# Matmul passes of the gate items, and the order of work at the start and end of each feed-forward block, in a two-layer fp32 decoder trunk

## The reference

```python
def swiglu(h, w_gate, w_up, w_down):
    return (jax.nn.silu(h @ w_gate) * (h @ w_up)) @ w_down

for l in range(DEPTH):                      # DEPTH = 2
    x = x + 0.5 * swiglu(rms_norm(x, g_ffn1[l]), w_ffn1_gate[l], w_ffn1_up[l], w_ffn1_down[l])
    h = rms_norm(x, g_mix[l])
    if l % 2 == 0:
        x = x + conv_gating_mixer(h, ...)   # causal convolution and spatial gating
    else:
        x = x + stick_breaking_mixer(h, w_qkv[i], w_o[i])   # 16 heads
    x = x + 0.5 * swiglu(rms_norm(x, g_ffn2[l]), w_ffn2_gate[l], w_ffn2_up[l], w_ffn2_down[l])
return rms_norm(x, g_final)
```

## Time and profile before

| | |
|---|---|
| Median of 3 runs | 1903.31 us (1903.06 to 1914.06) |
| The profiled execution | 1902.97 us, span of its instructions 1901.2 us |
| Mean granted TensorE clock | 0.993 of full speed |
| PE busy | 1843.3 us, 97% of the span, 11817 matmuls |
| PEld busy | 1646.3 us, 87% |
| DVE busy | 1408.8 us, 74% |
| ACT busy | 915.6 us, 48% |
| POOL busy | 504.6 us, 27% |
| DMA | 248.84 MB, mean 131 GB/s |

### The profile page before, as it was taken

One profiled execution on the slowest core, in us unless ns is written; L12 is line 12 of the kernel. 1 busy time (PEld: TensorE's weight loads), 2 busy tenths in 40 slices (PEclk: granted clock), 3 DMA queues, 4 the chain that ended last, 5 costly groups with the idle time before them and its releaser, 6 DMA issues.

```text
span 1901.2 us, 29396 instructions
## 1 busy us (share of the span) xinstructions
PE 1843.3 (97%) x11817; PEld 1646.3 (87%) x11817; DVE 1408.8 (74%) x1309; ACT 915.6 (48%) x1110; POOL 504.6 (27%) x379
## 2 busy tenths in 40 slices
PE   5999999999999999999999999999999999999997
PEld 5999988787779999887899988787888889999886
DVE  6797876589878888755888785654676688897753
ACT  6454544345274545444545453334565465455442
POOL 3344402201013433001344410221333224433021
PEclk8999999999999999999999999999999999999999
DMA  8788642232267886426778843222111277876321
GB/s 218 166 195 196 157 133 89 78 100 67 69 140 185 193 195 159 130 92 136 172 179 189 190 143 98 78 89 67 45 45 45 67 175 161 195 176 167 122 89 44
DMA packets 228250, 248.84 MB, mean 131 GB/s; under 512 B 7780, under 2 KB 196272, under 8 KB 227648
## 3 DMA queue, kind: packets, MB, share of 16 engines
q1 hardware_dynamic: 179232, 195.58, 34.0%
q0 software_dynamic: 48816, 51.98, 17.5%
q10 hardware_dynamic: 112, 0.03, 0.0%
HBM read 241.27 MB, written 2.10 MB: 128 GB/s over the span
## 4 chain that ended last, share of the span: by engine, by line
PE 74%; DVE 14%; issue 5%; ACT 3%; POOL 2%; DMA 1%; DVEq 0%; SPq 0%; ACTq 0%; POOLq 0%
PE ps L400 24%; PE ps L401 23%; PE ps L402 23%; DVE w_lo L1520 4%; DVE y L1814 2%; POOL chain L2144 2%; PE ps L903 1%; PE ps L897 1%; DVE xs_lo L1643 1%; ACT w_hi L1056 1%; DVE hid L1629 1%; DVE w_lo L1491 1%; PE ps L566 1%; DVE hid L1573 1%; DMA stage<-in_w_ffn_gate_dram 1%
## 5 line engine op out<-in xcount | busy, mean ns | idle before, releaser
L400 PE MATMUL ps<-xs_hi,w_hi 128*128 128x256 f32 (+1 forms) x3168 | 968.9, 306 | 37.3 <-DVE w_lo L1520 23.3
L401 PE MATMUL ps<-xs_lo,w_hi 128*128 128x256 f32 (+1 forms) x3168 | 963.8, 304 | 0.0
L402 PE MATMUL ps<-xs_hi,w_lo 128*128 128x256 f32 (+1 forms) x3168 | 963.6, 304 | 0.0
L400 PEld LDWEIGHTS ps<-xs_hi,w_hi 128*128 128x128 f32 x3168 | 598.5, 189 | 78.4 <-issue 30.9
L402 PEld LDWEIGHTS ps<-xs_hi,w_lo 128*128 128x128 f32 x3168 | 597.1, 188 | 31.9
L401 PEld LDWEIGHTS ps<-xs_lo,w_hi 128*128 128x128 f32 x3168 | 596.5, 188 | 32.4 <-issue 1.0
L1520 DVE TENSOR_TENSOR w_lo<-stage,w_hi 128x1024 fp32r<-128x1024 f32 x264 | 399.2, 1525 | 14.0 <-ACT w_hi L1056 13.0
L1056 ACT ACTIVATE w_hi<-stage 128x1024 fp32r<-128x1024 f32 x176 | 181.4, 1055 | 143.1 <-DMA stage<-in_w_ffn_gate_dram 74.0
L1643 DVE TENSOR_TENSOR xs_lo<-hid,xs_hi 128x1024 fp32r<-128x1024 f32 x88 | 110.5, 1255 | 176.0 <-ACT xs_hi L1176 176.0
L1520 DVE TENSOR_TENSOR w_lo<-chain,w_hi 128x1024 fp32r<-128x1024 f32 x132 | 160.9, 1219 | 87.3 <-ACT w_hi L1056 87.3
L1176 ACT ACTIVATE xs_hi<-hid 128x1024 fp32r<-128x1024 f32 x88 | 93.4, 1061 | 260.6 <-PE ps L402 254.7
(11 more groups left out here) (234 smaller groups left out, 2239.5 us busy)
## 6 DMA issues: line engine op xcount, KB each, us to landing
stage<-in_w_ffn_up_dram SPq DMA_DIRECT2D x88, 512.0 KB, 4.2
stage<-in_w_ffn_gate_dram SPq DMA_DIRECT2D x88, 512.0 KB, 6.2
stage<-in_w_ffn_down_dram SPq DMA_DIRECT2D x88, 512.0 KB, 3.8
chain<-in_w_ffn_gate_dram POOLq DMA_DIRECT2D x47, 512.0 KB, 7.5
stage<-in_w_ffn_gate_dram POOLq DMA_DIRECT2D x44, 512.0 KB, 8.8
chain<-in_w_ffn_up_dram SPq DMA_DIRECT2D x43, 512.0 KB, 7.4
stage<-in_w_qkv_dram SPq DMA_DIRECT2D x24, 512.0 KB, 4.7
stage<-in_w_in_ab_dram SPq DMA_DIRECT2D x16, 512.0 KB, 4.8
```

The lines of the kernel that those rows point to most:

```text
L400: pe.matmul(to, a_hi, b_hi, start=start, stop=False, skip_group_check=True)
L401: pe.matmul(to, a_hi, b_lo, start=False, stop=False, skip_group_check=True)
L402: return pe.matmul(to, a_lo, b_hi, start=False, stop=stop, skip_group_check=True)
```

## The change

1. **Gate items pass by pass.** `gate_part` becomes `gate_pass(..., part)`: part 0 is hi x hi for all t and k, part 1 is w_hi x xs_lo, part 2 is w_lo x xs_hi. `gate_item` waits for `item_hi_made` ahead of parts 0 and 1, and for `item_lo_made` only ahead of part 2. The number of matmuls stays.
2. **First step on PE.** `first_part` waits for each part on its own. The order was: W11 and T1 on tile groups 0 and 1, then W21 and T3 on tiles 0 to 2, then the last tile of all four. It is now: W11 and T1 on groups 0 and 1; T3 on tiles 0 to 2 (not in FFN 0); the last tile of T1 and W11; the rest of T3; all of W21.
3. **First step on ScalarE and VectorE** (`x_rest`, `gate_first`): T2 is split ahead of S2, v0 is copied and W22 split ahead of S4; T4's hi comes ahead of the squares of x tiles 4 to 7, which now follow T1 of step 1. In FFN 0 the copies of x tiles 4 to 7 move into `gate_first`. In FFN 1 and 3, T1 of step 0 is split earlier, between the x tiles.
4. **Step 2 on VectorE**: T3 and W21 of the next step are split at the end of a step, not at the start of the next; in `gate_second` they stand between `make_hid`, `c11` and `c22`.
5. **Down tail on PE**: outputs 4 and 5 are done row by row for the last two rows, outputs 6 and 7 as before.
6. **Attention on PE**: `suffix` runs on the hi half of `keep` before it waits for the lo half; `attend` runs its three passes over all key blocks in turn and waits for `prob_lo` only ahead of the last.

```diff
-            def gate_part(n, item, bank, ks):
+            def gate_pass(n, item, bank, ks, part):
 
                 slot = (RING_AT[n] + item) % RING
+                w, xs = (w_lo if part == 2 else w_hi), (xs_lo if part == 1 else xs_hi)
                 for t in range(2):
                     for k in ks:
...
+                        mm = pe.matmul(ps[:, bank + BANK_OF[item], t * HS:(t + 1) * HS],
+                                       w[:, slot, (2 * k + t) * P:(2 * k + t + 1) * P], xs[:, PART_OF[item], k, :],
...
             def gate_item(n, step, item):
 
-                pe.wait_ge(item_lo_made, step.count(ITEMS, n * FFN_ITEMS + item + 1))
+                pe.wait_ge(item_hi_made, step.count(ITEMS, n * FFN_ITEMS + item + 1))
...
-                gate_part(n, item, step.bank(n), range(KH)).then_inc(item_used, 1)
+                for part in range(2):
+                    gate_pass(n, item, step.bank(n), range(KH), part)
+                pe.wait_ge(item_lo_made, step.count(ITEMS, n * FFN_ITEMS + item + 1))
+                gate_pass(n, item, step.bank(n), range(KH), 2).then_inc(item_used, 1)
+
+            def first_part(n, item, ks, made):
+
+                bank = Step(0).bank(n)
+                pe.wait_ge(item_hi_made, n * FFN_ITEMS + item + 1)
+                pe.wait_ge(xs_hi_made, PARTS * n + made)
+                gate_pass(n, item, bank, ks, 0)
+                pe.wait_ge(xs_lo_made, PARTS * n + made)
+                gate_pass(n, item, bank, ks, 1)
+                pe.wait_ge(item_lo_made, n * FFN_ITEMS + item + 1)
+                return gate_pass(n, item, bank, ks, 2)
...
+                    first_part(n, W11, range(*PAIRS[g]), 2 * g + 1)
+                    first_part(n, T1, range(*PAIRS[g]), 2 * g + 2)
+                if n:
+                    first_part(n, T3, range(KH - 1), 2 * 2)
+                for item in (T1, W11):
+                    first_part(n, item, [KH - 1], 2 * len(PAIRS)).then_inc(item_used, 1)
+                first_part(n, T3, [KH - 1] if n else range(KH), 2 * len(PAIRS)).then_inc(item_used, 1)
+                first_part(n, W21, range(KH), 2 * len(PAIRS)).then_inc(item_used, 1)
...
-                for at in range(GROUP, DT):
+                for e in range(FT - TAIL, FT):
+                    down_ready(n, e)
+                    for at in range(GROUP, GROUP + 2):
+                        mm = down_item(n, e, at)
+                        if e == FT - 1:
+                            mm.then_inc(down_summed, 1)
+                for at in range(GROUP + 2, DT):
                     for e in range(FT - TAIL, FT):
...
-                pe.wait_ge(keep_lo_made, h + 1)
-                for part in (keep_hi, keep_lo):
+                for part, made in ((keep_hi, keep_hi_made), (keep_lo, keep_lo_made)):
+
+                    pe.wait_ge(made, h + 1)
```

More of the change, by code:

```diff
@@ L620, in gate_first @@
             def gate_first(n):
-                norm, step, bank = NORM_FFN[n], Step(0), Step(0).bank(n)
+                norm, step = NORM_FFN[n], Step(0)
                 pe.wait_ge(x_ready, norm * DT + GROUP)
                 for g in range(2):
[L625 to L637, removed]
@@ L639, in gate_first @@
+                for item in (T2, W22):
+                    pe.wait_ge(v0_copied if item == T2 else r0_copied, n * HF + 1)
+                    first_part(n, item, range(KH), 2 * len(PAIRS) + 1 + item - T2).then_inc(item_used, 1)
                 gate_item(n, step, T4)
@@ L1120, in gate_first @@
                 copy_r0(n, Step(0))
-                copy_v0(n, Step(0))
-                hi(n, Step(0), W22)
-                for j in range(GROUP, DT):
-                    x_square(n, j)
                 hi(n, Step(0), T4)
@@ L1127, in gate_first @@
                 hi(n, Step(1), T1)
+                for j in range(GROUP, DT):
+                    x_square(n, j)
                 hi(n, Step(1), W11)
@@ L1573, in make_hid, with x_copy @@
                 dve.tensor_tensor(hid[:, bass.ds(step.count(2, 0), 2), :], act_in[:, 0], act_in[:, 1], ALU.mult).then_inc(hid_made, 1)
+            def x_copy(j):
+                if j >= GROUP:
+                    dve.wait_ge(x_scaled, j // 2 + 1)
+                dve.wait_ge(turned, j + 1)
+                dve.tensor_copy(x_res[:, j, :], ps[:, (j + GROUP) % DT, :]).then_inc(x_ready, 1)
             def gate_first(n):
                 step = Step(0)
-                if n:
-                    lo(n, step, W22)
                 s57(n, step)
                 lo(n, step, T4)
+                if n == 0:
+                    for j in range(GROUP, DT):
+                        x_copy(j)
+                lo(n, step.next(), T1)
                 c11(n, step)
                 c22(n, step)
-                lo(n, step.next(), T1)
                 c12(n, step)
@@ L1602, in gate_second @@
                 make_hid(n, Step(0))
+                lo(n, step.next(), T3)
                 c11(n, step)
+                lo(n, step.next(), W21)
                 c22(n, step)
@@ L1609, in gate_step @@
             def gate_step(n, step):
-                lo(n, step, T3)
-                lo(n, step, W21)
                 make_hid(n, step.before())
@@ L1649, in to_down @@
                 end = Step(HF - 1)
-                lo(n, end, T3)
-                lo(n, end, W21)
                 make_hid(n, end.before())
@@ L1794, in _ @@
             x_rest(0)
-            lo(0, Step(0), W22)
-            for j in range(GROUP, DT):
-                x_copy(j)
             ffn(0)
@@ L1947, in _ @@
                 if j == 3:
+                    lo(1, Step(0), T1)
                     x_sum(1, 0)
```

43 lines of the change are left out of this document (20 added, 23 removed).

## The result

The changed kernel takes 1879.83 us (median of 4 runs, 1873.56 to 1886.03) and the kernel before 1903.18 us (4 runs, 1902.02 to 1914.06): ratio 0.9863, 95% interval 0.9838 to 0.9889. The profiled execution is 1877.12 us, 25.9 us under that of before; its span is 1875.4 us.

What follows compares the result with a forecast made beforehand. PE, busy for 97% of the span, bounds the kernel, so only pauses can go: 3.8 + 5.9 + 5.3 + 4.7 + 1.9 + 3.3 - 2.4 = 22.5 us from 1902.97 makes 1881 us, range 1873 to 1897.

Steps and rivals of the forecast that it cites:

- Openings: First step of each FFN: fewer PE pauses, 3.8 us gained in FFN 0 and 5.9 us in FFN 1 to 3.
- The hole in FFN 0: In FFN 0's opening, PE idles from 26.4 to 28.5 us until the last tile's parts come.
- The S4 pause: In the openings of FFN 1 to 3, W22's second pass waits 1.35 us for xs_lo of S4.
- Steps 2 and 3: T3's 2.15 us pause goes, W11's subtraction for step 3 ends at 97.1: 1.3 us for each FFN, 5.3 in all.
- Pitch: Behind the fp32 sum, starts 117.8 ns apart, not 113.3, last 240 matmuls, to step 3's W11: -2.4 us.
- the long stretches: Slow pitch in the FFN loops: as many matmuls as before, 1,480, one FFN's worth.
- my rival with two slow FFNs: Slow pitch persists where step 3's W11 doesn't stop PE: two FFNs slow give 1887 us; two or three, chance 0.28.
- Tails: Down tail: no wait at output 4's old time, outputs 5 to 7 come 1.3 us sooner; 4.7 us in all.
- attention: The keep_lo wait shrinks from 1.6 to 0.2 us and one smaller wait goes, taken as 0.5: 1.9 us.
- Clock: Two falls of the granted clock to half, about 3.4 us each, go with the pauses: 3.3 us gained.
- Broken stream: Rival: 308 more waits on PE, already met, cost 0.11 us each, 34 us, giving 1915 us; chance 0.06.

Runs made afterwards that it cites:

- t3_ahead: Changed kernel with T3 on tiles 0 to 2 ahead of the last tile in FFN 0 too; 1882.61 us.
- The square: Fp32 sum to step 4 without slow pitch: w_lo awaited ahead of item, old order 286.9 us, new 285.7, 285.5; ahead of third pass, 280.2, 280.7 and 277.8.
- tail_att: Kernel before with only the down tail's row order and attention's pass order changed (parts 5 and 6); 1900.37 us.
- gate_only: Kernel before with only the gate items outside the first step's first four going pass by pass, w_lo awaited ahead of the third; 1901.90 us.
- step2_only: Kernel before with only VectorE's splits of T3 and W21 moved to the end of the step before; 1913.80 us.

## Why the prediction was right, step by step

The forecast of 1881 us met 1879.83, but two of its terms were off, in opposite ways.

**Openings, right.** PE started at 20.52, not 20.05: I had W11's hi at its old time, and it came at 20.27, behind the split of T1. The hole in FFN 0 was 1.85 us between starts (2.1 expected), T2's pause and T4's were gone, and the seven items ended at 43.6 (43.3 expected). The stage is 5.6 us shorter, of which 1.5 is the half-clock stretch, so about 4.1 for the 3.8. FFN 2 had no hole at the last tile and gained 2.0 and not 1.3; FFN 1 had none and FFN 3 one of 0.4, where I had 0.8. The S4 pause was 1.0, 0.4 and 1.0 us against 1.35. GpSimd got the lock ahead of VectorE in all three, as argued. The Trainium skill's page "SBUF — State Buffer", section "SBUF: two separate sides", has the pair of ports go to whichever starts first. The record of starts here doesn't bear that out: in t3_ahead VectorE's subtraction shows its start 0.64 us ahead of GpSimd's addition and still took 4.67 us. Whether GpSimd held the ports before its recorded start no run shows.

**Steps 2 and 3, the step that was wrong.** I wrote that the subtraction of W11 for step 3, "which GpSimd again delays, ends at 97.1", and took 1.3 us for each FFN. In the changed kernel:

```profile
76.03 1.23 DVE L1594 TENSOR_TENSOR hid<-act_in 128x1024 f32 x1 [0.77 <-ACT act_in L1124]
77.22 1.23 DVE L1541 TENSOR_TENSOR w_lo<-chain,w_hi 128x1024 fp32r<-128x1024 f32 x1
...
87.85 1.22 DVE L1541 TENSOR_TENSOR w_lo<-stage,w_hi 128x1024 fp32r<-128x1024 f32 x1
...
90.64 3.80 DVE L1541 TENSOR_TENSOR w_lo<-stage,w_hi 128x1024 fp32r<-128x1024 f32 x2 [0.98 <-ACT w_hi L1074]
```

```profile
78.54 2.38 POOL L2164 TENSOR_TENSOR chain<-chain,stage 128x1024 f32<-128x1024 f32 x1 [10.23 <-DVE w_lo L1541]
...
89.78 2.45 POOL L2158 TENSOR_TENSOR chain<-chain,stage 128x1024 f32<-128x1024 f32 x1 [7.62 <-DMA stage<-in_w_ffn_gate_dram]
```

On this trace's clock, 5.63 us earlier than before's at the fp32 sum, T4's addition ends at 80.92 (86.55 on the old one, as predicted). But W11's subtraction ended at 89.07, which is 94.7 and not 97.1. GpSimd's next addition waited for its transfer until 89.78, so it missed W11 and met the splits of T3 and W21 for step 3, which are wanted only ahead of a third pass; T3's came 0.1 us late. I had moved VectorE's work and left GpSimd's at its old distance. The pauses of steps 2 and 3 went almost whole: 9.1 us and not 5.3. The square shows that the late wait brought most of it. That GpSimd's missed collision made the difference to 5.3 is read from this trace of FFN 0; no run moved GpSimd's addition alone.

**Pitch, right in kind, short in size.** The slow stretch behind the fp32 sum went from 120 matmuls to 168 in FFN 0 and 1 and 304 in FFN 2 and 3, which cost 2.1 us (2.4 expected; the recorded product of 130 x 4 x 4.45 ns is 2.3). It ended at step 2's T2 or step 3's T3 and never at step 3's W11, where I had it. For the long stretches I took as many as before, 1,480 matmuls, and got 2,240: 3.4 us more. In all that is 14.5 us of slow pitch against about 12. That is the condition of my rival with two slow FFNs, which I had put at 1887 us. Its mechanism wasn't what made them: no loop was slow because nothing stopped it behind the fp32 sum. FFN 1 came back quick at 594.9 and turned slow at a restart 0.05 us late at 610.6; FFN 2 turned at one 0.04 us late at 992.0.

**Tails, attention, right**: 4.6 for 4.7; attention 3.6 for 1.9 and a dip, of which tail_att alone gave 3.0 with none there. **Clock, about right**: 3.3 expected for two stretches. In FFN 0's opening 16 starts stood 213 ns apart instead of 118, which is 1.5 us; of attention's 3.6 us about 1.7 are left for the second when the 1.9 expected for its waits are taken off. There was a third before, in conv at 526.6, which I had missed: the stage is 0.4 us shorter without it. In most executions of the changed kernel conv has a half-clock stretch after its first pause, which takes 1.5 us back. **Broken stream**: 797 starts in 90 us with 33 waits that were already met among them; such waits cost nothing that can be seen.

So the 1881 came out with 3.8 us too little for the steps and 3.4 us of slow pitch in the long stretches that I had at nothing. That these two nearly cancel is luck, and so is which FFNs were slow in the profiled execution; the other terms held to 0.3 us, and the down rows, conv and the rest of steps 5 to 10 gave 1.7 us that I had at nothing.

## What to carry to other kernels

Where an operand is made in two halves by two engines, order the passes so that the late half is used last, and wait for it there: that was worth 6 to 8 us here in the steps behind the sum, and reordering the maker's work 1 to 3. When one engine's work is moved, move what hangs on it on every other engine too, transfers included, before counting a collision as kept. Where a stream has two rates that are drawn at each restart, count the matmuls in fixed windows and take that part out before a single run is compared with another; gate_only and step2_only would otherwise have read as no gain and a loss.
